# Constant products on TensorE inside and after the sums of five layer norms

## The chip, the cores and the metric

The program runs on one core of a Trainium2 chip, in one launch. The metric is the device time in microseconds (us), from the start of the execution to its end. Five engines run side by side, each with its own instruction stream, and they wait for one another through semaphores: TensorE (PE in the profile, its weight loads PEld), VectorE (DVE), ScalarE (ACT), GpSimd (POOL) and SyncE (SP), which issues most of the loads from the chip's memory.

## The reference, cut to what matters

Two transformer stacks follow one another on one sequence of 256 tokens with 1024 features, all in float32. The first has four layers (three kinds of attention, RMS norms, SwiGLU) and a closing RMS norm. The second has two layers, and its norms are layer norms. There are five of them: one on the way in, and two in each layer.

```
def layer_norm(x, g, b):
    mu = jnp.mean(xf, axis=-1, keepdims=True)
    var = jnp.mean(jnp.square(xf - mu), axis=-1, keepdims=True)
    y = (xf - mu) * lax.rsqrt(var + LN_EPS) * g + b

def second_block(x, ...):
    h = layer_norm(x, ln_in_g, ln_in_b)
    for l in range(DEPTH_2):                      # 2 layers
        mix = token_mix(h, ...)                   # products, pool, conv, attention, gates
        h = layer_norm(DEEPNORM_ALPHA * h + mix, ln1_g[l], ln1_b[l])
        ffn = conv_ffn(h, ...)
        h = layer_norm(DEEPNORM_ALPHA * h + ffn, ln2_g[l], ln2_b[l])
    return h
```

## The kernel before, in words

Activations are kept transposed: 1024 features as 8 tiles of 128 partitions, 256 tokens along the free axis (`xT`, `hT`). A matrix product in float32 is made of three products of rounded parts, high by high, low by high and high by low (`product`, L421 to L426). The weights stream in units of 128 by 2048 elements through three slots: SyncE loads a unit, ScalarE makes its high part (L1272), VectorE its low part (L1700), and TensorE waits for `lo_ready` (`next_unit`). A slot is refilled once its unit has been multiplied. In each deep product one refill, that of its last unit, is held back until the norm behind it is done (the list `late`).

Every engine's order is fixed by the order in which its own function issues the work. On TensorE a wait holds back everything that is written behind it.

A layer norm runs like this.

1. TensorE: `sums(at, xT, ...)` multiplies an all-ones matrix by the 8 tiles of `xT`, which leaves the column sums, spread over all partitions, in a bank. It waits before each pair of tiles.
2. VectorE: four additions centre `xT`, two tiles at a time (L2062).
3. ScalarE: four squares of the centred pairs into `sq` (L1532).
4. TensorE: `sums(at + 1, sq, ...)`, again 8 multiplications, with a wait for each pair of squares.
5. ScalarE: the square root (L1333). VectorE: the reciprocal (L2069), then for each tile the scaled value `hT` (L2074) and, two tiles behind, the low part `h_lo` (L2078). ScalarE makes the high part `h_hi` between them, and afterwards the shifted `xT` (both L1538).
6. TensorE: the next product. Its first unit waits for each of the 8 tiles of `h_lo` in turn (`gate` in `tiles`), and does six multiplications with each, 48 in all. Behind the last norm it is the transposes of the output instead (L1089), in two groups that wait for tiles 0 to 3 and 4 to 7 of `xT`.

The banks are the 8 banks of TensorE's accumulator memory. A norm behind a token mix uses banks 0 and 1, the others banks 4 and 5. `open_item(bank)` waits until all earlier uses of the bank have been released, and `close` lets a multiplication increment `pe_done`, for which the readers wait. `sums` is used by the five layer norms and, once, by the closing RMS norm of the first stack. In the profile it is line L529 and all multiplications by the weights are L426.

Of the kernel before, what the change touches and what calls it, by code (L numbers as in the profile page):

```python
# [33 lines left out]
T = 256  # L34
# [77 lines left out]
def build(nc, t, stages=99):  # L112

    with ExitStack() as ctx:
        def sb(name, shape, dt=F32, where=None):
            return (where or ctx).enter_context(nc.sbuf_tensor(name, shape, dt))

        def sem(name):
            return ctx.enter_context(nc.semaphore(name))
# [9 lines left out]
        sq = sb("sq", [P, KT, T])  # L129
        pres = sb("pres", [P, 6 * T])  # L130
        rots = sb("rots", [P, 4 * T])
        tab = sb("tab", [P, 6, T])
        rotm = sb("rotm", [P, 3, P])
        ident = sb("ident", [P, P])
        ones = sb("ones", [P, P])
# [17 lines left out]
        banks = [ctx.enter_context(nc.psum_tensor(f"bank{b}", [P, 512], F32)) for b in range(BANKS)]  # L153
# [64 lines left out]
        bank_free = [sem(f"bank_free{b}") for b in range(BANKS)]  # L218
# [20 lines left out]
        squares_ready = sem("squares_ready")  # L239
# [139 lines left out]
        def _(pe):  # L379
            n_done = [0]  # L380
            uses = [0] * BANKS
            tally = {}

            def count(s, n=1):

                tally[s.name] = tally.get(s.name, 0) + n
                return tally[s.name]

            def open_item(bank, released=True):

                if uses[bank]:
                    pe.wait_ge(bank_free[bank], uses[bank])
                uses[bank] += released
                return Item(bank, uses[bank])

            def close(ins, *what):

                n_done[0] += 1
                ins.then_inc(pe_done, 1)
                for w in what:  # L400
                    w.done = n_done[0]
# [118 lines left out]
                    items[norm[0]].append(b)  # L520
                    norm[0] = None

            def sums(bank, src, ready):

                x = open_item(bank)
                for j in range(KT):
                    if j % 2 == 0:
                        ready(j // 2)
                    mm = nc.tensor.matmul(banks[bank][:, 0:T], ones[:], src[:, j, :], start=(j == 0), stop=(j == KT - 1))  # L529
                close(mm, x)  # L530
                return x

            def final():
                x = sums(6, sq, lambda j: pe.wait_ge(squares_ready, count(squares_ready)))
                items["final"] = [x]
# [404 lines left out]
            def ln(tag, source):  # L940

                at = 0 if source and source[0].bank else 4
                if source:
                    m = sums(at, xT, lambda j: pe.wait_ge(bank_free[source[j].bank], source[j].free))
                else:
                    m = sums(at, xT, lambda j: pe.wait_ge(y_ready, 2 * j + 2))
                v = sums(at + 1, sq, lambda j: pe.wait_ge(squares_ready, count(squares_ready)))
                count(ln_ready, KT)
                items[tag] = m, v

# [145 lines left out]
            for kind, arg in phases():  # L1096
                if kind == "start":
                    start()
                elif kind == "rms":
                    norm[0] = arg  # L1100
                elif kind == "A":
                    attn_a(arg)
                elif kind == "B":
                    attn_b(arg)
                elif kind == "C":
                    attn_c(arg)
                elif kind == "ffn":
                    ffn("f_w_gu", "f_w_out", arg, ("ffn", arg))
                    last_add[0] = (("ffn", arg), "down")
                elif kind == "rows2":  # L1110
                    rows2()
                elif kind == "final":
                    final()
                elif kind in ("ln", "ln_last"):
                    ln(arg, None if arg[0] == "ln_in_g_2" else items[last_add[0]])
                elif kind == "mix":
                    mix(arg)
                    last_add[0] = (("m", arg), "wo")
                elif kind == "ffn2":
                    ffn("w_up_2", "w_down_2", arg, ("ffn2", arg))  # L1120
                    last_add[0] = (("ffn2", arg), "down")
                elif kind == "end":
                    end()
# [1279 lines left out]
```

## Time and profile before

| | |
|---|---|
| median of 3 runs | 2566.22 us (2564.52 to 2566.51) |
| profiled execution | span 2564.6 us from the first to the last instruction |
| TensorE busy | 2427.2 us (95%), 18456 multiplications |
| VectorE, ScalarE, GpSimd busy | 1536.9 us (60%), 1137.7 us (44%), 343.6 us (13%) |
| mean granted TensorE clock | 0.952 of full speed |
| chain of waits that ended last | TensorE 83%, VectorE 6%, GpSimd 6%, ScalarE 3% |

The profiled execution's time outside its span is not shown separately. Its span is 1.6 us below the median of the runs. "Granted clock" is a share of full speed: 1.0 is 2.4 GHz, 0.5 is 1.2 GHz. A float32 multiplication of `sums` appears in the trace as two records, so that 8 multiplications are x16. Ends of multiplications are modelled and overlap their successors; the distance from one start to the next is the one that adds up.

### The profile page before, as it was taken

Reading aid. Unit: us, or ns where it says so; the run is one execution under the profiler, and the core shown is the slowest. Engines: PE = TensorE matmul, PEld = TensorE weight load, DVE = VectorE, ACT = ScalarE, POOL = GpSimd, SP = SyncE. Lnnn points to the kernel's source line nnn. Section 1 sums busy time; section 2 is a strip of 40 time slices with the busy share of each in tenths; the row PEclk is TensorE's granted clock in tenths of the full one; section 3 lists DMA queues with packets and bytes.
Section 4 is the critical chain, followed back from the end, with each engine's and each line's share of the span. In section 5 each row is a group of like instructions: output and inputs, shape, how many; then the busy total and the mean of one; then the engine's idle time right before and its main releaser. Section 6 shows DMA issues by size and latency. Waiting matters only on the chain.

```text
span 2564.6 us, 46394 instructions
## 1 busy us (share of the span) xinstructions
PE 2427.2 (95%) x18456; PEld 2305.0 (90%) x18456; DVE 1536.9 (60%) x1906; ACT 1137.7 (44%) x1477; POOL 343.6 (13%) x448
## 2 busy tenths in 40 slices
PE   8899998999989999999998999899899999988998
PEld 7799997799979997999996999789689988968998
DVE  5746546565445557465565554578667648766764
ACT  4543344543344345433345433434455444444552
POOL 0002100022000000021020110191001109200210
PEclk9989998999989998999998999999799999989999
DMA  6327543166535450265551565345246545423652
GB/s 217 116 66 197 180 146 115 48 166 180 190 119 167 164 166 25 67 181 183 176 167 57 157 188 183 99 127 169 65 126 183 184 129 152 147 81 111 186 190 73
DMA packets 431030, 361.99 MB, mean 141 GB/s; under 512 B 20524, under 2 KB 404144, under 8 KB 430904
## 3 DMA queue, kind: packets, MB, share of 16 engines
q1 hardware_dynamic: 429128, 358.79, 45.5%
q8 instruction: 90, 1.47, 0.2%
q0 software_dynamic: 1264, 0.71, 0.1%
q10 hardware_dynamic: 512, 0.72, 0.1%
q14 instruction: 36, 0.29, 0.0%
HBM read 359.12 MB, written 1.05 MB: 140 GB/s over the span
## 4 chain that ended last, share of the span: by engine, by line
PE 83%; DVE 6%; POOL 6%; ACT 3%; issue 1%; DMA 1%; SPq 0%; ACTq 0%; DVEq 0%; POOLq 0%
PE bank L426 70%; POOL hT L1234 3%; PE bank L752 2%; PE bank L766 2%; POOL Z L1236 2%; PE bank L457 2%; PE bank L540 2%; PE bank L658 2%; DVE weights_lo L1700 2%; PE bank L529 2%; ACT weights_hi L1272 1%; PE bank L464 1%; DVE negmax L1887 1%; DVE V L1903 0%; DVE sq L2069 0%
## 5 line engine op out<-in xcount | busy, mean ns | idle before, releaser
L426 PE MATMUL bank<-h_hi,weights_hi 128*128 128x256 f32 (+1 forms) x3920 | 1145.5, 292 | 40.5 <-DVE h_lo L2078 16.6
L1700 DVE TENSOR_TENSOR weights_lo<-weights,weights_hi 128x2048 fp32r<-128x2048 f32 x343 | 789.6, 2302 | 642.6 <-ACT weights_hi L1272 640.7
L426 PE MATMUL bank<-h_lo,weights_hi 128*128 128x256 f32 (+1 forms) x3920 | 1123.4, 287 | 0.0
L426 PE MATMUL bank<-h_hi,weights_lo 128*128 128x256 f32 (+1 forms) x3920 | 1123.0, 286 | 0.0
L1272 ACT CAST weights_hi<-weights 128x2048 fp32r<-128x2048 f32 x343 | 652.7, 1903 | 588.7 <-PE bank L426 579.9
L426 PEld LDWEIGHTS bank<-h_hi,weights_hi 128*128 128x128 f32 (+1 forms) x3920 | 766.4, 196 | 56.9 <-issue 47.9
L426 PEld LDWEIGHTS bank<-h_lo,weights_hi 128*128 128x128 f32 (+1 forms) x3920 | 766.5, 196 | 10.4 <-issue 10.3
L426 PEld LDWEIGHTS bank<-h_hi,weights_lo 128*128 128x128 f32 (+1 forms) x3920 | 765.6, 195 | 0.0
L426 PE MATMUL bank<-hid_hi,weights_hi 128*128 (+1 forms) x1056 | 295.4, 280 | 0.0
L426 PE MATMUL bank<-hid_lo,weights_hi 128*128 (+1 forms) x1056 | 295.4, 280 | 0.0
L426 PE MATMUL bank<-hid_hi,weights_lo 128*128 (+1 forms) x1056 | 295.4, 280 | 0.0
L1185 POOL CAST hid_hi<-hT 128x256 f32 (+1 forms) x132 | 52.4, 397 | 1683.1 <-DVE hT L2040 1241.4
L426 PEld LDWEIGHTS bank<-hid_hi,weights_hi 128*128 128x128 f32 x1056 | 198.5, 188 | 0.0
L426 PEld LDWEIGHTS bank<-hid_lo,weights_hi 128*128 128x128 f32 x1056 | 198.5, 188 | 0.0
L426 PEld LDWEIGHTS bank<-hid_hi,weights_lo 128*128 128x128 f32 x1056 | 198.5, 188 | 0.0
L1187 POOL TENSOR_TENSOR hid_lo<-hT,hid_hi 128x256 f32 (+1 forms) x132 | 114.4, 867 | 19.7 <-POOL hid_hi L1185 17.7
L2031 DVE TENSOR_TENSOR pres<-bank,hT 128x512 f32<-128x512 f32 x88 | 60.8, 691 | 84.9 <-PE bank L426 84.8
L426 PE MATMUL bank<-weights_hi,h_hi 128*128 128x256 f32 (+2 forms) x360 | 107.2, 298 | 0.0
L426 PE MATMUL bank<-weights_lo,h_hi 128*128 128x256 f32 (+2 forms) x360 | 102.4, 284 | 0.0
L426 PE MATMUL bank<-weights_hi,h_lo 128*128 128x256 f32 (+2 forms) x360 | 102.4, 284 | 0.0
L1234 POOL TENSOR_SCALAR hT<-Z,pcol 128x256 f32<-128x256 f32 x60 | 88.6, 1477 | 0.0
L1620 ACT ACTIVATE pres<-bank,pcol 128x256 f32<-128x256 f32 x88 | 44.9, 560 | 97.9 <-PE bank L426 97.9
(262 smaller groups left out, 2483.7 us busy)
## 6 DMA issues: line engine op xcount, KB each, us to landing
weights<-in_f_w_gu SPq DMA_DIRECT2D x176, 512.0 KB, 4.9
weights<-in_f_w_out SPq DMA_DIRECT2D x88, 512.0 KB, 4.2
weights<-in_w_up SPq DMA_DIRECT2D x88, 512.0 KB, 4.9
weights<-in_w_in SPq DMA_DIRECT2D x82, 512.0 KB, 4.4
weights<-in_c_w_qkv SPq DMA_DIRECT2D x72, 512.0 KB, 4.3
weights<-in_a_w_qkv SPq DMA_DIRECT2D x48, 512.0 KB, 4.5
weights<-in_w_down SPq DMA_DIRECT2D x44, 512.0 KB, 4.0
weights<-in_a_w_o SPq DMA_DIRECT2D x16, 512.0 KB, 4.2
```

The source lines that it names most:

```text
L426: mm = nc.tensor.matmul(out, x, y, start=(first and n == 0), stop=(last and n == 2), skip_group_check=True)
L457: mm = nc.tensor.matmul(banks[bank][:, col + tt:col + tt + 1], src[:, j, tt * P:(tt + 1) * P], ones[:, 0:1], start=(n == 0), stop=(n == le ...
L529: mm = nc.tensor.matmul(banks[bank][:, 0:T], ones[:], src[:, j, :], start=(j == 0), stop=(j == KT - 1))
L540: close(nc.tensor.matmul(banks[r.bank][lo:hi, 0:n], rotm[lo:hi, m, lo:hi], pre[x.pre][lo:hi, 0:n], start=True, stop=True), r)
L658: mm = nc.tensor.transpose(banks[it.bank][:, b:b + P], expos[hd % 3][:, a:a + P], ident[:])
L752: mm = nc.tensor.matmul(banks[s.bank][:, a:b], lhsT, rhs, start=True, stop=True)
L1185: gp.tensor_copy(hid_hi[:, at], hT[:, j, :]).then_inc(hid_step, 1)
L1187: gp.tensor_tensor(hid_lo[:, at], hT[:, j, :], hid_hi[:, at].bitcast(F32), ALU.subtract).then_inc(hidden_ready, 1)
L1234: gp.tensor_scalar(hT[:, 2 + j % 2, :], hh, wj, None, ALU.mult).then_inc(conv_step, 1)
L1272: nc.scalar.copy(w_hi[slot][:], raw[slot][:]).then_inc(hi_ready, 1)
L1700: v_.tensor_tensor(w_lo[slot][:], raw[slot][:], w_hi[slot][:].bitcast(F32), ALU.subtract).then_inc(lo_ready, 1)
L2031: free(v_.tensor_tensor(pre[j].rearrange("p (m n) -> p m n", m=2), banks[x.bank][:].rearrange("p (m n) -> p m n", m=2), hT[:, 4, :].unsque ...
```

## The change

The diff adds a helper `busy(n)` that multiplies the all-ones matrix by a constant table (`tab[:, 0, :]`, cosines loaded at the start) into bank 7, n times. Its results are read by nobody. It waits once for the earlier uses of bank 7 to be released. The line is L527 after the change, and the line of `sums` becomes L535.

```
+            def busy(n):
+
+                pe.wait_ge(bank_free[7], uses[7])
+                for _ in range(n):
+                    nc.tensor.matmul(banks[7][:, 0:T], ones[:], tab[:, 0, :], start=True, stop=True)
+
-            def sums(bank, src, ready):
+            def sums(bank, src, ready, fill=0):
 
                 x = open_item(bank)
                 for j in range(KT):
                     if j % 2 == 0:
                         ready(j // 2)
                     mm = nc.tensor.matmul(banks[bank][:, 0:T], ones[:], src[:, j, :], start=(j == 0), stop=(j == KT - 1))
+                    if fill and j % 2:
+                        busy(fill)
                 close(mm, x)
                 return x
@@ in ln(tag, source)
-                v = sums(at + 1, sq, lambda j: pe.wait_ge(squares_ready, count(squares_ready)))
+                busy(3)
+                v = sums(at + 1, sq, lambda j: pe.wait_ge(squares_ready, count(squares_ready)), fill=2)
+                busy(7)
```

What this does to TensorE's order is seen at the second of the five norms, the one behind the first token mix. `bank` stands for any bank; `xT,ones` are the sums of step 1, `sq,ones` those of step 4. Before:

```order
L426 MATMUL bank<-h_hi,weights_hi 128x256
L426 MATMUL bank<-h_lo,weights_hi 128x256
L426 MATMUL bank<-h_hi,weights_lo 128x256
L529 MATMUL bank<-xT,ones 128x256 x8
L529 MATMUL bank<-sq,ones 128x256 x8
L426 MATMUL bank<-h_hi,weights_hi 128x256
```

The same place after the change, where `tab,ones` are the added multiplications:

```order
L426 MATMUL bank<-h_hi,weights_lo 128x256
L535 MATMUL bank<-xT,ones 128x256 x8
L527 MATMUL bank<-tab,ones 128x256 x3
L535 MATMUL bank<-sq,ones 128x256 x2
L527 MATMUL bank<-tab,ones 128x256 x2
L535 MATMUL bank<-sq,ones 128x256 x2
L527 MATMUL bank<-tab,ones 128x256 x2
L535 MATMUL bank<-sq,ones 128x256 x2
L527 MATMUL bank<-tab,ones 128x256 x2
L535 MATMUL bank<-sq,ones 128x256 x2
L527 MATMUL bank<-tab,ones 128x256 x9
L426 MATMUL bank<-h_hi,weights_hi 128x256
```

The eight multiplications of the squares now stand in four pairs with two added ones behind each pair; the last two are written together with the seven of `busy(7)`, as nine. Three stand ahead of the first pair.

The last of the five norms, before and then after, with the transposes of the output behind it:

```order
L426 MATMUL bank<-hid_hi,weights_lo 128x256
L529 MATMUL bank<-xT,ones 128x256 x8
L529 MATMUL bank<-sq,ones 128x256 x8
L1089 MATMUL bank<-ident,xT 128x128 x16
L114 UNCONDITIONAL_BRANCH
```

After the change:

```order
L426 MATMUL bank<-hid_hi,weights_lo 128x256
L535 MATMUL bank<-xT,ones 128x256 x8
L527 MATMUL bank<-tab,ones 128x256 x3
L535 MATMUL bank<-sq,ones 128x256 x2
L527 MATMUL bank<-tab,ones 128x256 x2
L535 MATMUL bank<-sq,ones 128x256 x2
L527 MATMUL bank<-tab,ones 128x256 x2
L535 MATMUL bank<-sq,ones 128x256 x2
L527 MATMUL bank<-tab,ones 128x256 x2
L535 MATMUL bank<-sq,ones 128x256 x2
L527 MATMUL bank<-tab,ones 128x256 x9
L1099 MATMUL bank<-ident,xT 128x128 x16
```

Here the nine stand ahead of the transposes. Nothing moves on another engine.

## Rows read from the trace of the kernel before

**Rows 1.** The page: the chain that ended last, by engine and by line.
```profile
PE 83%; DVE 6%; POOL 6%; ACT 3%; issue 1%; DMA 1%; SPq 0%; ACTq 0%; DVEq 0%; POOLq 0%
PE bank L426 70%; POOL hT L1234 3%; PE bank L752 2%; PE bank L766 2%; POOL Z L1236 2%; PE bank L457 2%; PE bank L540 2%; PE bank L658 2%; DVE weights_lo L1700 2%; PE bank L529 2%; ACT weights_hi L1272 1%; PE bank L464 1%; DVE negmax L1887 1%; DVE V L1903 0%; DVE sq L2069 0%
```

**Rows 2.** Chain of waits through the third norm: start us, us, what.
```profile
2086.23 3.47 PE bank L529 x16
...
2089.72 0.70 DVE xT L2062
...
2090.45 0.64 ACT sq L1532
...
2091.22 3.71 PE bank L529 x16
...
2094.95 0.48 ACT sq L1333
...
2095.45 1.76 DVE sq L2069
...
2097.24 1.28 DVE hT L2074 x3
2098.52 0.41 DVE h_lo L2078
...
2099.06 8.99 PE bank L426 x55
```

**Rows 3.** Instructions in order of time, same norm: start us, us, engine, line [idle before].
```profile
2090.45 2.42 ACT L1532 ACTIVATE sq<-xT 128x512 f32<-128x512 f32 x4 [6.39 <-DVE xT L2062]
...
2091.22 3.69 PE L529 MATMUL bank<-sq,ones 128*128 128x256 f32 x16 [1.54 <-ACT sq L1532]
```

**Rows 4.** In order of time: TensorE's first work behind the second and the last norm.
```profile
1895.83 0.55 PE L426 MATMUL bank<-h_hi,weights_hi 128*128 128x256 f32 x1 [4.15 <-DVE h_lo L2078]
...
2556.92 3.67 PE L1089 MATMUL bank<-ident,xT 128*128 128x128 f32 x16 [4.61 <-ACT xT L1538]
```

**Rows 5.** Stretches: length, busy us (xcount) of PE, PEld, DVE, ACT, POOL, clock, DMA.
```profile
1622.80:1629.50 6.70, 5.18 (x12) 4.17 (x13) 3.71 (x9) 0.00 (x0) 0.00 (x0) 0.50 0.48 154
1629.70:1639.70 10.00, 4.59 (x21) 3.40 (x19) 5.78 (x9) 3.92 (x8) 0.00 (x0) 1.00 0.01 2
...
1892.00:1895.70 3.70, 0.00 (x0) 0.00 (x0) 3.44 (x6) 1.36 (x4) 0.00 (x0) 1.00 0.00 0
1895.90:1899.10 3.20, 3.20 (x15) 3.20 (x16) 3.20 (x9) 2.03 (x4) 0.00 (x0) 0.50 0.00 0
...
2097.30:2103.90 6.60, 4.84 (x23) 4.87 (x24) 6.36 (x16) 4.73 (x11) 0.00 (x0) 0.50 0.01 1
...
2554.70:2561.00 6.30, 3.67 (x16) 3.24 (x16) 5.64 (x12) 3.30 (x8) 0.00 (x0) 0.50 0.05 22
```

**Rows 6.** In order of time: 48th and 49th multiplication behind the second norm; 49th behind the third.
```profile
1903.03 0.28 PE L426 MATMUL bank<-h_hi,weights_lo 128*128 128x256 f32 x1
1903.15 0.28 PE L426 MATMUL bank<-h_hi,weights_hi 128*128 128x256 f32 x1
...
2107.05 0.28 PE L426 MATMUL bank<-h_hi,weights_hi 128*128 128x256 f32 x1
```

**Rows 7.** In order of time: the first two and the last three `h_lo` behind the second norm.
```profile
1895.20 0.48 DVE L2078 SCALAR_TENSOR_TENSOR h_lo<-hT,pcol,h_hi 128x256 fp32r<-128x256 f32 x1
...
1896.00 0.48 DVE L2078 SCALAR_TENSOR_TENSOR h_lo<-hT,pcol,h_hi 128x256 fp32r<-128x256 f32 x1
...
1899.16 1.27 DVE L2078 SCALAR_TENSOR_TENSOR h_lo<-hT,pcol,h_hi 128x256 fp32r<-128x256 f32 x3
```

**Rows 8.** In order of time: VectorE at the end of the program.
```profile
2554.64 3.26 DVE L2074 SCALAR_TENSOR_TENSOR hT<-xT,pcol,sq 128x256 f32<-128x256 f32 x8
...
2560.63 0.69 DVE L2316 COPY Q<-bank 128x512 f32<-128x512 f32 x1 [0.16 <-PE bank L1089]
```

**Rows 9.** In order of time: the held-back refill behind the second norm, on VectorE.
```profile
1904.82 2.29 DVE L1700 TENSOR_TENSOR weights_lo<-weights,weights_hi 128x2048 fp32r<-128x2048 f32 x1 [4.39 <-ACT weights_hi L1272]
```

## The prediction

> **What bounds the kernel now.** I read the chain of waits first. TensorE carries 83% of it, and the multiplications by the weights alone 70% [rows 1]. What TensorE loses or wins at a norm is therefore lost or won by the end, unless something else is late anyway. The 6% of GpSimd are no such cover. They lie in the token mixes, behind the third unit of the product that follows a norm, so they move with the norm.
>
> Next I read the chain through one norm, in order of time [rows 2]. Everything in it is serial: sums of `xT` on TensorE, the first centring on VectorE, the first square on ScalarE, 3.7 us of sums of the squares on TensorE, the root, the reciprocal, three scalings and the first `h_lo`, then the next product. The other four norms show the same pieces within 0.1 us, but for the first, whose sums of `xT` run partly at the lower clock, and the last, which ends in transposes.
>
> Then I read what TensorE waits for. It stands idle twice, 1.54 us for the first square [rows 3] and 4.15 us for the first `h_lo`, or 4.61 us before the transposes [rows 4]. Between the two it doesn't wait. ScalarE needs 2.42 us for all four squares, and TensorE 3.69 us for their sums [rows 3], so that only the first square is waited for.
>
> Last I read the granted clock by stretches. While TensorE stands still behind the second norm the clock is 1.00, and as the product begins it is 0.50, that is 1.2 GHz, for 3.2 us and more [rows 5]. In the third norm the lower clock begins earlier, 2.3 us after the sums, and lasts until 2103.9 [rows 5]. Each of the five norms is followed by such a stretch. The change is aimed at these.
>
> **The price of one added multiplication.** It has the shape and types of those in the sums, of which 16 records take 3.69 us, the last with 0.38 us of modelled length (the duration of one record at 2.4 GHz). So (3.69 − 0.38)/15 = 0.221 us from record to record, and a multiplication of two records takes 0.441 us. At 1.2 GHz twelve records took 5.18 us [rows 5], which is 0.86 us for one.
>
> **Part one, three ahead of the squares.** 3 × 0.441 = 1.32 us. From the last record of the first sums to the first of the next there are 0.38 + 1.54 = 1.92 us, of which 0.22 are the last record's own, so 1.70 us are open. They fit. Cost 0. At 1.2 GHz they would take 2.6 us and cost 0.9 us; the sums of `xT` ran at the full clock right ahead of this gap in all five, so I keep 0.
>
> **Part two, two behind each pair of squares.** TensorE works in order, and these stand ahead of real work that is already possible. Three of the four groups stand ahead of the last real multiplication, on which the root waits: 6 × 0.441 = 2.65 us for each norm. No idle time hides them, since the squares arrive faster than they are summed. With 4 multiplications per pair TensorE needs 1.77 us where ScalarE brings a pair in 0.6. The root, the reciprocal, `hT`, `h_lo` and the product are queued behind in a chain [rows 2], and all are 2.65 us later. In five norms 13.2 us. From below, this can be nothing only if they did not delay the real ones; from above, at 1.2 GHz, it is 6 × 0.86 = 5.2 us.
>
> **Part three, nine behind the last pair.** 9 × 0.441 = 3.97 us. Open are 0.38 + 4.15 − 0.22 = 4.31 us, ahead of the transposes 4.77 [rows 4]. They fit with 0.3 us to spare, so cost 0. Nine at 1.2 GHz would take 7.7 us and cost 3.4.
>
> **The added waits.** `busy` waits for bank 7. Behind a token mix, bank 7 holds a quarter of the last product, but the sums of `xT` already wait for its release before their fourth pair, and `busy` stands behind them. At the other norms the bank was released long before. Behind each such wait TensorE's whole stream is queued, but none of them lasts. Cost 0.
>
> **What the clock gives back.** With the gaps filled, I expect TensorE to enter the product at 2.4 GHz. The trace bears out that multiplications of this very kind raise the clock: the sums of `xT` in the first norm ran at 0.50 until about 1629.6, and went on at 1.00 [rows 5].
>
> Behind the second norm the first unit's 48 multiplications took from 1895.83 [rows 4] to the 49th at 1903.15 [rows 6], 7.32 us. At full clock they are 0.12 us apart [rows 6], which would be 5.76 us. But the unit is fed by VectorE: the `h_lo` tiles end at 0.79 us intervals for the first six and 0.40 for the last two [rows 7]. Six multiplications take 0.72 us, less than 0.79, so tile by tile TensorE waits for VectorE until the sixth tile, which comes 1899.16 − 1895.20 = 3.96 us after the first. Three tiles are then left: 3.96 + 3 × 0.72 = 6.12 us. The gain is 7.32 − 6.12 = 1.20 us. The first and the fourth norm took 7.25 and 7.31 us by the same reading and give 1.13 and 1.19. The third took 2107.05 [rows 6] − 2099.06 [rows 2] = 7.99 us and gives 1.87. Without the feeding limit the gains would be 0.36 us more in each.
>
> Behind the last norm the transposes run at 0.50 for 3.67 us [rows 5], and the last copy out of their banks ends at 2561.32 [rows 8]. At full clock a bank would fill in about 0.5 us, half of 0.86, so the four copies would be limited by VectorE, which is free at 2557.90 [rows 8]: 4 × 0.71 later is 2560.74. Gain 0.6 us. Together 1.13 + 1.20 + 1.87 + 1.19 + 0.6 = 6.0 us. The bounds are 0 (clock not held) and 8.6 (nothing but the clock limits: four times 0.36 more, and 1.8, half of 3.67, at the end).
>
> What is late next? The unit whose refill is held back. Its low part is ready at 1904.82 + 2.29 = 1907.11 [rows 9], 11.28 us after the product's start, and it is the third unit. With a first unit of 6.12 and a second of 48 × 0.12 = 5.76 us it is wanted at 11.88 us. It stays hidden with 0.6 us to spare.
>
> **The sum.** 13.2 − 6.0 = +7.2 us. The profiled execution's span of 2564.6 becomes 2571.8. What lies around the span is unchanged, and the median stood 1.6 us above this span, so the time is 2566.2 + 7.2 = 2573.4 us. With the bounds of the gain the net lies between +4.6 (13.2 − 8.6) and +13.2.
>
> **A rule that decides the sign.** The records of the sums stand in program order and evenly spaced [rows 3], which does not show whether a waiting stream could be overtaken. The Trainium skill, "TensorE: Matmul & The Clock Gate", section "The mechanism", says that only weight loads are pulled ahead, and that multiplications start and end strictly in program order. By that rule the added ones inside the sums are paid in full. Without it they would be filled in only where TensorE is free, and the first rival below would hold.
>
> **The rivals.**
> 1. *The fillers inside the sums don't delay them, and only the clock's gain is left.* The price of part two would be 0 and the time 2566.2 − 6.0 = 2560.2, faster. The kernel gets faster from the point at which an added multiplication ahead of the root costs under 6.0/30 = 0.20 us (six in each of five norms). For it: nothing but that the loads of the all-ones matrix might be saved. Against it: equal shapes at a steady 0.221 us per record, where TensorE and not the squares is the limit. 5%.
> 2. *The constants don't hold the clock.* No gain, 13.2 us of cost, and where the clock falls while the nine run they overrun. In the third norm it fell 2.4 us after the point where the nine would begin. Then 5.5 of them at 0.441 and 3.5 at 0.86 us take 5.4 us, against 4.31 open, +1.1. Time 2566.2 + 14.3 = 2580.5. For it: nothing in the trace shows this operand. Against it: the same kind of work raised the clock in the first norm. In a sentence apart: the same page of the Trainium skill, section "What's actually happening", says that the clock follows how busy the array has been recently, and names no dependence on operands for that; by it this rival fails. 8%.
> 3. *The gain is larger than the feeding limit allows, or part two is partly hidden.* Six added ones at 0.35 instead of 0.441 us, or a product fed faster, either worth the 2.6 us between 8.6 and 6.0. Net +4.6 us, 2570.8. Against it: both limits are read from rows that repeat in every norm. 12%.
> 4. *The later norms shift the low-clock stretches elsewhere in the token mixes* by a microsecond or two in either direction. That only widens the forecast.
>
> **How the numbers follow.** The forecast, 2573.4, has 75% with a range of its own of 2570.5 to 2576. The 80% range reaches to rival 3 and part of the way to rival 2, and takes in the spread of 2 us between runs: 2568.5 to 2578. A measurement can tell about 0.2%, 5.1 us, from no change. The forecast case lies above 2571.3 nine times in ten and rival 2 always, slower 0.74. Rival 3 and the rest of the forecast give no change, 0.21. Rival 1 gives faster, 0.05.
>
> **What would show it.** In the profile after, the sums of the squares should stretch from 3.69 to about 6.4 us from first to last real record, the root should start right behind them, and the product should begin 4.15 us later than the sums' end as before, with a granted clock of 1.0. The first unit should take 6.1 us from its first start to the 49th. Between norms nothing should differ. I am wrong if the product starts at 0.50, if the nine overrun and the product starts more than 4.2 us behind the last real sum, if a wait for `weights_lo` appears at the third unit, or if the norm's span from the first sum to the product grows by less than 2.5 us.

## The result, and the profile after

The changed kernel takes 2570.57 us (median of 10 runs, 2569.47 to 2572.26) against 2564.39 us before (10 runs, 2561.14 to 2566.51). The ratio is 1.0025, 95% interval 1.0016 to 1.0034: slower by 6.2 us, where 7.2 were forecast. As a time the forecast was 2573.4 us, 2.8 us above the measured one: 1.8 of these lie in the kernel before, whose median was 2566.2 us over the three runs that the forecast started from, and 1.0 in the change.

The chain of waits through the third norm, after the change (start us, us, what), to be read beside [rows 2]:

```profile
2088.34 0.70 DVE xT L2072
...
2089.07 0.64 ACT sq L1542
...
2089.84 1.10 PE bank L535 x4
2090.95 0.86 PE bank L527 x4
2091.81 0.86 PE bank L535 x4
2092.67 0.86 PE bank L527 x4
2093.53 0.86 PE bank L535 x4
2094.40 0.86 PE bank L527 x4
2095.26 0.88 PE bank L535 x4
...
2096.16 0.48 ACT sq L1343
...
2096.67 1.76 DVE sq L2079
...
2098.46 1.28 DVE hT L2084 x3
2099.74 0.41 DVE h_lo L2088
...
2100.28 7.84 PE bank L426 x61
```

The constants (L527) now stand in the chain itself, three times 0.86 us. That is 2.59 us, or 0.432 us for each of the six. The other pieces have the length they had. The idle time ahead of each reciprocal on VectorE tells the same in one number: 3.25 us before, 5.84 after, in all five norms.

```profile
1892.05 1.75 DVE L2079 RECIPROCAL sq<-sq 128x256 f32<-128x256 f32 x1 [5.84 <-ACT sq L1343]
```

The start of the product and its 49th multiplication, after the change, in order of time:

```profile
2100.28 0.36 PE L426 MATMUL bank<-h_hi,weights_hi 128*128 128x256 f32 x1 [0.27 <-DVE h_lo L2088]
...
2106.39 0.28 PE L426 MATMUL bank<-h_hi,weights_hi 128*128 128x256 f32 x1
```

TensorE is idle for 0.27 us where it was 4.15 [rows 4], and the first unit takes 6.11 us instead of 7.99 [rows 2, 6]. The other three first units take 6.11, 6.13 and 6.12. The stretches of that place show why. Columns are length, busy us of PE, PEld, DVE, ACT and POOL, granted clock, DMA:

```profile
2096.50:2100.20 3.70, 3.51 (x17) 2.75 (x15) 3.50 (x6) 1.36 (x4) 0.00 (x0) 1.00 0.00 0
2100.40:2103.40 3.00, 3.00 (x25) 2.93 (x25) 3.00 (x9) 2.00 (x4) 0.00 (x0) 1.00 0.00 0
...
2561.00:2564.00 3.00, 2.12 (x16) 1.71 (x16) 2.89 (x7) 1.92 (x5) 0.00 (x0) 1.00 0.00 0
```

The clock is 1.00 where it was 0.50 [rows 5], at the end of the program too.

To see where the difference of the two profiles arises, I took the start of the reciprocal in each norm (one instruction each) and the end of the span, and subtracted neighbours. The spans themselves (2564.6 and 2568.2) differ by only 3.6 us, because the first stack, in which nothing changed, happened to be 2.5 us shorter in the profiled execution after. Spans are known to 0.1 us, and so is the last column.

| us from reciprocal to reciprocal | mix 1 | feed-forward 1 | mix 2 | feed-forward 2 | to the end |
|---|---|---|---|---|---|
| before | 255.85 | 203.23 | 254.18 | 203.22 | 11.7 |
| after | 255.53 | 204.62 | 256.02 | 204.62 | 10.9 |
| difference | −0.32 | +1.39 | +1.84 | +1.39 | −0.8 |

To these comes the first norm, from its first sum to its reciprocal, +2.63. The sum is +6.1, which agrees with the medians.

### The profile page after: what moved, and what is told of

It reads as the page before. It is cut to its first block, busy times and chain, and to the rows that moved or that the text cites. A ratio compares the mean times of both kernels' runs of the same rounds, so it can differ in the third digit from the quotient of the medians.

```text
span 2568.2 us, 46754 instructions
## 1 busy us (share of the span) xinstructions
PE 2455.2 (96%) x18636; PEld 2329.7 (91%) x18636; DVE 1535.7 (60%) x1906; ACT 1137.2 (44%) x1477; POOL 344.2 (13%) x448
## 4 chain that ended last, share of the span: by engine, by line
PE 83%; DVE 6%; POOL 6%; ACT 3%; issue 1%; DMA 1%; SPq 0%; ACTq 0%; DVEq 0%; POOLq 0%
PE bank L426 70%; POOL hT L1244 4%; PE bank L760 2%; PE bank L774 2%; POOL Z L1246 2%; PE bank L457 2%; PE bank L548 2%; DVE weights_lo L1710 2%; PE bank L535 2%; PE bank L666 2%; ACT weights_hi L1282 1%; PE bank L464 1%; DVE negmax L1897 1%; PE bank L527 1%; DVE V L1913 0%
```

## The experiments

In all kernels below, the sums of `xT` in the first norm and everything ahead of them are as in the change, unless it is said otherwise, and an edit holds for all five norms. A step is the time from one reciprocal to the next.

**The six inside the sums taken out.**

```
-                v = sums(at + 1, sq, lambda j: ..., fill=2)
-                busy(7)
+                v = sums(at + 1, sq, lambda j: ...)
+                busy(9)
```

> The six added multiplications that stand ahead of the last real sum of each norm are taken out; three stay ahead of the squares and nine behind the last pair, so that 12 of 18 remain. Theory (the price is in the six, the gain in the clock that the others hold): the sums of the squares take 3.7 us again, the product still starts at full clock and its first unit takes 6.1 us, so the time is 6 us below before (ratio 0.9977) and 12 us below the change. Rival (the added ones cost wherever they stand, or the clock is held only with those inside the sums): the time is that of before or above it, ratio 1.000 or more.

Measured: 2558.53 us against 2565.22, ratio 0.9977 (0.9967 to 0.9987). The stretches of the third norm in this kernel, ahead of and behind the product's start at 2094.26:

```profile
2090.30:2094.20 3.90, 3.69 (x18) 2.90 (x16) 3.51 (x6) 1.56 (x4) 0.00 (x0) 1.00 0.00 0
2094.30:2097.30 3.00, 3.00 (x24) 2.95 (x24) 3.00 (x9) 1.92 (x4) 0.00 (x0) 1.00 0.00 0
```

The clock holds just as well, the sums take 3.69 us, the first units 6.12 or 6.13, and the feed-forward steps 202.03 us: 1.20 below before, 2.59 below the change. The theory stands. The same idea is faster than before once it stays off the path. By how much is less sure: the profile's steps across the mixes are 252.34 and 251.91 us, and all five steps together are 9.0 us shorter than before. The first units and the end explain 6.2 of them. The other 2.8 lie inside the mixes, 2.4 of them in mix 1, where the clock was low for a shorter time. The section on the prediction comes back to that.

**The part inside the sums alone.**

```
-                busy(3)
...
-                busy(7)
```

> The opposite part alone: two added ones behind each pair of squares, none ahead of the sums and only those two behind the last pair. Theory: the sums take 6.3 us, then TensorE stands still for over 3 us, the clock falls again in every norm and the first unit takes 7.2 us or more: before plus 13 us, ratio 1.005. Rival (the work inside the sums holds the clock by itself, the nine behind are not needed): plus 7 us, ratio 1.0027, with the product at a granted clock of 1.0.

Measured: 2576.38 us against 2565.22, ratio 1.0046 (1.0031 to 1.0062). In order of time, TensorE in the third norm of this kernel, and then two stretches:

```profile
2094.63 1.03 PE L527 MATMUL bank<-tab,ones 128*128 128x256 f32 x4
...
2098.95 0.55 PE L426 MATMUL bank<-h_hi,weights_hi 128*128 128x256 f32 x1 [3.29 <-DVE h_lo L2086]
```

```profile
2095.80:2098.90 3.10, 0.00 (x0) 0.00 (x0) 3.06 (x6) 1.25 (x3) 0.00 (x0) 0.96 0.00 0
2099.00:2102.00 3.00, 3.00 (x14) 3.00 (x15) 3.00 (x9) 1.92 (x4) 0.00 (x0) 0.50 0.00 0
```

The sums pay, and the clock falls all the same: in this norm 0.3 us ahead of the product, in the other three 0.5 to 0.7 us behind its start. First units take 7.2 to 7.3 us. So the work inside the sums holds no clock for what comes 3.3 us later. Its feed-forward steps are 205.84 and 205.81, 2.6 us above before, which is the price of the six and nothing else.

**Four instead of two inside.**

```
-                v = sums(..., fill=2)
-                busy(7)
+                v = sums(..., fill=4)
+                busy(5)
```

> The change with four instead of two added ones behind each pair of squares, and still nine in all behind the last pair. Theory (each one ahead of the last real sum costs its full 0.43 to 0.44 us): sums of the squares 8.9 us, 13 us above the change, ratio to before 1.0075. Rival (the price of the change is a fixed cost of breaking up the sums and its waits, not of the number): same time as the change, 1.0025.

Measured: 2581.31 us against 2565.22, ratio 1.0058 (1.0043 to 1.0074). The runs are 10 us above the change instead of 13, with four runs that spread over 7 us. The profile is sharper. The chain through its third norm:

```profile
2099.01 1.10 PE bank L535 x4
2100.11 1.73 PE bank L527 x8
2101.84 0.86 PE bank L535 x4
2102.70 1.73 PE bank L527 x8
2104.43 0.86 PE bank L535 x4
2105.29 1.73 PE bank L527 x8
2107.02 0.88 PE bank L535 x4
```

Three times 1.73 us, so the price is proportional to the number and there is no fixed part. Feed-forward steps 207.20 and 207.21, 2.59 us above the change, as the change's own step is 2.59 above that of the kernel without the six (202.03).

**Four instead of nine behind.**

```
-                v = sums(..., fill=2)
-                busy(7)
+                v = sums(...)
+                busy(4)
```

> Three added ones ahead of the squares, none between the pairs, four instead of nine behind them, so that TensorE stands still for about 2.5 us ahead of the product. Theory: half of the gap filled still holds the clock in most norms, 3 to 6 us below before. Rival (the whole pause has to be filled): the clock falls in every norm as before, time as before, ratio 1.000.

Measured: 2563.88 us against 2565.22, ratio 0.9992 (0.9983 to 1.0001). Third norm, stretches ahead of and behind the product's start:

```profile
2094.20:2096.40 2.20, 0.00 (x0) 0.00 (x0) 2.17 (x6) 1.14 (x3) 0.00 (x0) 1.00 0.00 0
2096.60:2098.00 1.40, 1.40 (x12) 1.40 (x12) 1.40 (x5) 0.88 (x2) 0.00 (x0) 1.00 0.05 12
2098.20:2099.60 1.40, 1.40 (x8) 1.40 (x8) 1.40 (x5) 0.90 (x2) 0.00 (x0) 0.50 0.00 0
```

My theory was wrong here. The four end 2.4 us ahead of the product (which starts at 2096.56), the clock is still 1.00 through the pause, and 1.5 us later it falls although TensorE is at work again. In the other three norms it falls within 0.3 us of the product's start, ahead of it in the first two, so that nearly the whole first unit is slow:

```profile
1893.40:1896.40 3.00, 3.00 (x14) 3.00 (x15) 3.00 (x9) 1.91 (x4) 0.00 (x0) 0.50 0.02 5
```

First units take 7.19, 7.29, 7.40 and 7.31 us; only the third is better than before (7.99). A pause that is filled in its first half is worth almost nothing.

**Also behind the closing RMS norm.** Beside the version with three ahead and nine behind, ten constants behind the sums of the first stack's last norm:

```
                 items["final"] = [x]
+                busy(10)
```

> As the kernel with three ahead of the squares and nine behind them, none between, and in addition ten added multiplications behind the sums of the first stack's closing RMS norm, where TensorE stands still for 4.8 us ahead of the first layer norm's sums. Theory: ten take 4.4 us and fit in the 4.95 us that are open, the clock stays at 1.0, and the first norm's sums of xT take 3.6 instead of 6.1 to 6.3 us: another 2.5 us, 8.5 us below before, ratio 0.9967. Rival (the ten overrun or the closing norm's VectorE chain is what is late): 0.9977 as without them.

Measured: 2555.65 us against 2563.60, ratio 0.9964 (0.9952 to 0.9976), the lowest time of all. Stretches ahead of the first norm and during its first sums:

```profile
1619.00:1622.00 3.00, 2.59 (x12) 1.93 (x11) 2.96 (x5) 0.00 (x0) 0.00 (x0) 1.00 0.46 115
1622.10:1625.70 3.60, 3.60 (x17) 3.19 (x18) 2.20 (x6) 0.00 (x0) 0.00 (x0) 1.00 0.56 190
```

The mechanism works: the sums of `xT` take 3.69 us at full clock instead of 6.1 to 6.3. But the gain is not shown. The ratio's interval overlaps that of the version without it, and in the profile the step across mix 1 is 254.87 us, 2.53 more than the 252.34 there, so the profiled execution gave all of it back. The section on the prediction says where. There is no second profile of this kernel.

**Nothing ahead of the squares.** Only the nine behind:

```
-                busy(3)
                 v = sums(...)
                 busy(9)
```

> Only the nine behind the squares; none ahead of them and none between. Theory: the 1.5 us pause ahead of the squares never cost the clock anything (the squares' sums ran at full clock before the change), so the nine do all the work: ratio 0.9977, first units 6.1 us. Rival (the three are needed as well): some products start at 0.50 and the time is 1 to 4 us more than that.

Measured: 2559.94 us against 2563.60, ratio 0.9983 (0.9974 to 0.9993). First units 6.11 to 6.13 us, and all steps within 0.1 us of those with the three (252.33, 202.03, 251.94, 202.02, and to the end 10.9). The three ahead of the squares do nothing. The pause they fill, 1.54 us [rows 3], never cost the clock. In the third norm of this kernel, the pause ahead of the squares and the sums behind it:

```profile
2087.20:2088.70 1.50, 0.00 (x0) 0.01 (x1) 1.48 (x3) 0.76 (x2) 0.00 (x0) 1.00 0.00 0
2088.80:2092.30 3.50, 3.50 (x17) 3.09 (x18) 0.90 (x2) 1.56 (x3) 0.00 (x0) 1.00 0.00 0
```

**Twenty behind.** In the version with three ahead of the squares and none between.

```
-                busy(9)
+                busy(20)
```

> Three ahead, none between, twenty instead of nine behind the squares. Theory: the pause is open for 4.3 us and each added one takes 0.43 to 0.44, so that the product starts 20 x 0.435 - 4.3 = 4.4 us late in each norm. Part of it comes back in the first unit, since VectorE has all tiles of h_lo ready by then (the last is there 4.75 us after the first): the unit takes 5.8 us instead of 6.1. Net 4.1 us in each of four norms and 4 in the last, against the nine 20 us more, 14 us above before, ratio 1.0055. Rival (the product overtakes the constants, which are then free in any number): 0.9977.

Measured: 2579.64 us against 2563.60, ratio 1.0051 (1.0036 to 1.0065). In order of time, TensorE in the third norm:

```profile
2100.01 8.80 PE L527 MATMUL bank<-tab,ones 128*128 128x256 f32 x40
2108.45 0.47 PE L426 MATMUL bank<-h_hi,weights_hi 128*128 128x256 f32 x1
```

The product stands behind the constants and starts 8.28 us after the last real sum instead of 4.15. It doesn't overtake. Feed-forward steps 205.98, 3.95 above the nine (4.1 expected), with first units of 5.93 to 5.95 us.

**Zeros instead of cosines.** In the version with three ahead and nine behind; `idle` is a tile whose first column holds zeros.

```
-   nc.tensor.matmul(banks[7][:, 0:T], ones[:], tab[:, 0, :], start=True, stop=True)
+   nc.tensor.matmul(banks[7][:, 0:T], ones[:], idle[:, 0:1].to_broadcast([P, T]), start=True, stop=True)
```

> Three ahead and nine behind, none between, with a column of zeros broadcast along the tokens as the moving operand instead of the table of cosines. Theory: what the constants are does not matter for the granted clock: first units 6.1 us at 1.0, ratio 0.9977. Rival (the clock follows the operands' data): with zeros it falls as before, ratio 1.000.

Measured: 2557.42 us against 2563.60, ratio 0.9968 (0.9955 to 0.9981). Third norm, behind the product's start:

```profile
2094.50:2097.50 3.00, 3.00 (x24) 2.96 (x24) 3.00 (x9) 1.91 (x4) 0.00 (x0) 1.00 0.00 0
```

First units take 6.11 to 6.13 us, and the steps are within 0.1 us, but for 0.11 in mix 2, of those of the version with cosines. Multiplying by zeros holds the clock too.

**The same two kernels again.** The kernel before and the changed one, not edited, two more profiles of each.

> The kernel before, unchanged, profiled again. Theory (what is left between the forecast and the measured time is chance in the two token mixes, whose low-clock stretches start at another point in each execution): the steps from norm to norm across the feed-forward parts stay 203.2 us within 0.1, and those across the token mixes differ from 258.5 and 254.2 by 1 to 4 us with the same code. Rival (the mixes are as exact as the rest and the change did something in them): both steps repeat within 0.3 us.

> The kernel before, unchanged, a third profile. Theory: feed-forward steps 203.2 us, mix steps spread by 1 to 4 us. Rival: mix steps repeat within 0.3 us.

> The changed kernel, profiled again. Theory: feed-forward steps 204.6 us within 0.1, mix steps spread by 1 to 4 us around 258.2 and 256.0. Rival: mix steps within 0.3 us of these.

> The changed kernel, a third profile. Theory: feed-forward steps 204.6 us, mix steps spread by 1 to 4 us. Rival: mix steps repeat within 0.3 us.

| step, us | mix 1 | feed-forward 1 | mix 2 | feed-forward 2 | to the end |
|---|---|---|---|---|---|
| before, again | 255.90 | 203.18 | 254.04 | 203.23 | 11.7 |
| before, third | 255.75 | 203.21 | 254.05 | 203.25 | 11.7 |
| change, again | 255.45 | 204.61 | 256.07 | 204.61 | 10.9 |
| change, third | 255.64 | 204.61 | 255.97 | 204.63 | 10.9 |

The times of these four single runs are 2563.64, 2568.19, 2574.51 and 2569.83 us.

The theory fell and the rival holds: the mixes repeat within 0.2 us in the same code. What differs from one execution to the next lies ahead of the layer norms. The first reciprocal comes at 1633.75, 1636.37 or 1638.38 us in the kernel before, and all five steps together differ by 0.2 us. In the changed kernel it comes at 1636.52, 1641.02 or 1636.23.

## Why the prediction was right, point by point

- **Part two, the six ahead of the last real sum**, was forecast at 2.65 us a norm and is 2.59. The record distance in the stream is 0.216 us, not the 0.221 that I had taken from the first and last start of a group with a modelled length. In five norms 13.0 instead of 13.2. Shown by the chain, and by four instead of two.
- **Parts one and three** cost nothing, as forecast. The nine end 0.27 us ahead of the product. With twenty the overrun appears at once.
- **The clock's gain in the first unit** was forecast at 1.13, 1.20, 1.87 and 1.19 us. The units take 6.11 to 6.13 us against 6.12, so that the gains are 1.14, 1.19, 1.88 and 1.19. That VectorE's `h_lo` sets this floor, and not TensorE, is borne out by the twenty: with more tiles ready at the start the unit takes 5.94.
- **The end** was forecast to gain 0.6 us and gained 0.8. The limit was the one named, VectorE's four copies behind its scalings. They took 2.68 us where I had counted 2.8, and the first began 0.1 us ahead of the modelled end of the last scaling. The 0.5 us for filling a bank should have read 0.43, half of 0.86; nothing hung on it. In the rows, the first is the kernel before and the other two are the change:

```profile
2552.85 1.75 DVE L2069 RECIPROCAL sq<-sq 128x256 f32<-128x256 f32 x1 [3.25 <-ACT sq L1333]
2557.31 1.75 DVE L2079 RECIPROCAL sq<-sq 128x256 f32<-128x256 f32 x1 [5.84 <-ACT sq L1343]
2562.27 2.68 DVE L2326 COPY Q<-bank 128x512 f32<-128x512 f32 x4
```

From the reciprocal to the end of the last copy this is 8.47 us before (2561.32 [rows 8]) and 7.64 after.

- **The added waits and the held-back refill** did not show, as forecast. No wait for `weights_lo` appears at the third unit.
- **The token mixes** were forecast to carry the norm's difference unchanged ("between norms nothing should differ"). That is wrong, and the fourth rival, which let low-clock stretches shift there by a microsecond or two in either direction, is what happened. Mix 1 should have grown by 2.59 − 1.14 = 1.45 us and shrank by 0.32; mix 2 should have grown by 2.59 − 1.88 = 0.71 and grew by 1.84. The two misses are −1.8 and +1.1 us, and they nearly cancel: together 0.6 us in the change's favour. With the 0.3 of the price and the 0.2 of the end this is the distance between 7.2 and 6.1. That they cancel was luck, since the sum had no term for either. The shifts themselves are not scatter between executions, since they repeat.

Where it lies in the mix is seen by the clock over the attention part, from its first scores to the last product. First the kernel before (mix 1, mix 2), then the change:

```profile
1800.10:1843.70 43.60, 40.10 (x192) 27.87 (x192) 23.10 (x48) 19.31 (x48) 0.00 (x0) 0.76 0.06 18
2260.30:2301.00 40.70, 37.33 (x192) 26.51 (x192) 23.10 (x48) 19.02 (x48) 0.00 (x0) 0.82 0.06 19
```

```profile
1800.10:1841.00 40.90, 37.36 (x192) 26.44 (x193) 23.09 (x48) 19.19 (x48) 0.00 (x0) 0.82 0.06 19
2260.50:2301.60 41.10, 37.56 (x192) 26.63 (x192) 23.09 (x48) 19.23 (x48) 0.00 (x0) 0.82 0.07 21
```

The same 192 records take 43.6 us at a mean clock of 0.76, or about 41 at 0.82. This part is full of short pauses, and its low-clock stretch lasts 27.3 or 20.5 us. Inside it, in mix 1, before and then after:

```profile
1793.60:1820.50 26.90, 22.02 (x65) 13.88 (x64) 16.14 (x33) 14.89 (x36) 0.00 (x0) 0.50 0.15 54
1794.60:1814.80 20.20, 15.91 (x49) 10.47 (x49) 13.52 (x28) 12.66 (x30) 0.00 (x0) 0.50 0.14 54
```

The change turned the long one in mix 1 into the short one, 2.7 us less. A second place takes something back. Where the gates' product resumes behind a wait for weights, the clock over the following stretch is 0.78 and 0.77 before, and lower after the change:

```profile
1742.20:1750.00 7.80, 7.80 (x53) 7.80 (x53) 7.42 (x17) 0.09 (x1) 0.00 (x0) 0.78 0.61 188
2202.60:2210.00 7.40, 7.40 (x49) 7.40 (x50) 7.05 (x16) 0.00 (x0) 0.00 (x0) 0.77 0.58 173
```

```profile
1741.80:1750.00 8.20, 8.20 (x51) 8.20 (x52) 7.78 (x18) 0.00 (x0) 0.00 (x0) 0.71 0.64 198
2202.00:2210.00 8.00, 8.00 (x47) 8.00 (x48) 7.58 (x18) 0.00 (x0) 0.00 (x0) 0.66 0.62 193
```

The low stretch there lasts 6.8 instead of 3.4 us, and it costs 0.4 us in mix 1 and 0.9 in mix 2 from the resumption to the first scores (57.93 and 57.66 us before, 58.32 and 58.59 after). The rest is small: in mix 1 GpSimd's convolution gives back 0.55 of the 1.13 us won ahead of it, and in mix 2 the attention takes 0.17 us more. With these, mix 1 is 2.71 − 0.39 − 0.55 = 1.77 us better than the norm alone would make it, and mix 2 is 0.93 + 0.17 = 1.10 worse. The long attention stretch is also what took back the gain behind the closing norm. In that kernel:

```profile
1794.20:1837.90 43.70, 40.22 (x192) 27.98 (x193) 23.09 (x48) 19.28 (x48) 0.00 (x0) 0.76 0.06 21
```

I have shown that the length of the low-clock stretch in a part with many short pauses differs between kernels whose code for this part is the same, and that it repeats within one kernel. What makes it long or short is open. It is not how long after the start of the execution the part comes: the first norm came up to 4.8 us earlier or later in the same kernel, and the stretch was the same. Nor is it the code of the norms alone: the kernel with the ten has the same five norms as the version with three ahead and nine behind, and its stretch in mix 1 is the long one where the other has the short one. So something further ahead has a part in it.

Of the rivals, the first (the constants don't delay) is refuted by the chain and by the twenty. The second (constants don't hold the clock) is refuted by every kernel with nine, and by the zeros. The third (a larger gain, or part two partly hidden) had 2570.8 us, nearly the measured 2570.57, but not for its reason: an added multiplication cost 0.432 us and not 0.35, and no first unit was faster than 6.11. The measured time also lies only 0.1 us inside the forecast's own range of 2570.5 to 2576, since the median before came out 1.8 us lower and the mixes gave 0.6.

The rule named in the prediction, that multiplications keep program order (the Trainium skill, "TensorE: Matmul & The Clock Gate", section "The mechanism"), agrees with this case: the 20 constants, 40 records, delayed the product by 4.13 us, from 4.15 to 8.28.

## What to carry to other kernels

Filler work for the clock belongs only where the engine would stand still, behind the last instruction for which anyone waits: here nine multiplications behind the sums gained 1.1 to 1.9 us a norm ahead of a product and 0.8 at the end, and six in front of their end cost 2.6. Fill the pause whole: four instead of nine, at the start of the pause, gained next to nothing. Numbers between four and nine, or four placed later in the pause, were not tried.

## What the runs showed of the hardware that was not expected

- After a pause of 2.4 us the clock was, in the third norm, still at 2.4 GHz when the product began, and fell to 1.2 GHz 1.5 us later (four behind). After 3.3 us it did so 0.5 to 0.7 us later in three of four norms (the part inside alone). A clock that is full at the start of the work doesn't prove that the pause was harmless.
- A moving operand of zeros, read with a broadcast of one column, holds the clock as well as a table of cosines does (first units 6.11 to 6.13 us).
- Between executions of one kernel, the second stack repeats within 0.2 us of 928, while the time ahead of it varies by 4.6 us (first reciprocal at 1633.75 to 1638.38). To compare variants, steps between fixed instructions of one profile told apart 0.1 us, where the intervals of the ratios are 2 us and more to either side.
